# One decoder layer, prompt and decode together: meta tokens as keys and values only

## The chip, the cores and the metric

The kernel runs on one core of a Trainium2 chip, as one program that its author wrote out engine by engine, with semaphores by hand. The metric is the device time of one launch in microseconds. Engines are named as the profile names them: PE (TensorE, matmuls), PEld (its weight loads), ACT (ScalarE), DVE (VectorE), POOL (GpSimd, here mostly a DMA issuer), SP (SyncE, the other DMA issuer).

## The reference

One layer, D = 2048, 16 query heads and 4 key/value heads of 128, for two groups of tokens that share the weights: a prompt of 512 tokens with 16 learned meta tokens in front of it (528 positions), and 8 decode tokens with paged caches of 2048 positions each.

```
h = rmsnorm(x);  sq,sk,sv, fq,fk,fv, fl, g_sb,g_fx = split(h @ w_in)     # 12 parts of one projection
fq, fk = rmsnorm per head;  log_f = log_sigmoid(fl + b)
o_sb = stick_breaking(sq, sk, sv)      # strictly causal: exp(log_sigmoid(z) + suffix sum of -softplus(z))
o_fx = softmax(fq fk' * s + cum_q - cum_k) fv      # causal, bias from cumulative log forget
x += (sigmoid(g_sb) * o_sb + sigmoid(g_fx) * o_fx) @ w_out
x += relu(rmsnorm(x) @ w_up)^2 @ w_down            # D_FF = 8192
outputs: y for the 512 prompt tokens (y_prompt = x[:, 16:]) and the 8 decode tokens;
         sk, sv, fk, fv, log_f for all 528 prompt positions and the 8 decode tokens
```

The results that belong to a meta token alone (its queries, gates, attention output, residual, feed-forward) are not among the outputs. Its keys, values and forget logs are outputs, and all prompt queries attend to them.

## The kernel before, in words

All 536 tokens (16 meta, 512 prompt, 8 decode) lie along the free axis of every activation, features along partitions. A weight slab is 2048 x 128 (or, for the down projection, 1024 x 256), loaded in 1 MB by SP, split by ACT (`split_hi`) and DVE (`split_lo`) into a rounded high part and a rest, both float32r. A product is three matmuls into one PSUM bank (`split3`: high*high, low*high, high*low). `dense` runs a slab: 16 row blocks by two halves of HT = 268 columns, so 96 matmuls. The down projection's slab has the same count.

The stages, in PE's order:

- load and transpose x, first norm, four key/value groups of four slabs (`keys_values`), the forget slab, the first query slab;
- 16 stick-breaking heads (m = 0), then 16 forgetting heads (m = 1), function `head` on each engine. A head has one slab of the next head's queries (sq) and one of its own gates (sg), and between parts of these the attention: `scores` for five query tiles of 128 rows (aligned to position 0, so tile 0 has the meta tokens and the last tile 16 rows), each against `KW[i]` keys, with a floor of 256 columns; a bf16 mask matmul on the diagonal block; for m = 1 two more matmuls that add the forget bias. ACT and DVE turn scores into weights in `Z` (the stick-breaking chain in two parts, `Z_PARTS`: tiles 0 to 2 and tiles 3 and 4). `turn` transposes `Z` in six groups of blocks of at most 128 x 128; ACT and DVE split each group out of PSUM (`pa_hi`, `pa_lo`, `pb_hi`, `pb_lo`). `values` multiplies them with V: query tiles 0 and 1 as 256 columns over 2 key blocks, tiles 2 to 4 as 272 columns over 5;
- the decode tokens' attention over their caches (not touched);
- `wout`, the second norm, and eight chunks of the feed-forward (up slabs, down slabs), all through the same split products; at the end 20 transposes of four per 128 tokens and the stores.

`s_free`, `s_ok`, `pt_ps`, `pt_hi`, `pt_lo`, `o_ok` count how far PE, ACT and DVE are with a head; each engine takes its instructions strictly in written order, so an engine that waits holds all behind it.

Of the kernel before, what the change touches and what calls it, by code (L numbers as in the profile page):

```python
# [23 lines left out]
AX_X = mybir.AxisListType.X  # L24

# [11 lines left out]
HT = T // 2  # L37
KT = D // P
# [62 lines left out]
def build(nc, x_prompt, x_sample, cache_sb_k, cache_sb_v, cache_fox_k, cache_fox_v, cache_fox_logf,  # L101
# [3 lines left out]
    with ctx:  # L105
# [9 lines left out]
        xT_dram = nc.dram_tensor("xT_dram", [P, KT, T], F32).ap()  # L115
        kT_dram = nc.dram_tensor("kT_dram", [2 * NKV, P, TP], F32).ap()
        start_dram = nc.dram_tensor("start_dram", [1, 4], F32).ap()
        mg_dram = nc.dram_tensor("mg_dram", [2 * NH, P, TP], F32).ap()
# [44 lines left out]
        qraw = sb("qraw", [P, T], where=early)  # L163
        kraw = sb("kraw", [P, TP], where=early)
        vraw = sb("vraw", [P, TT, HD], where=early)
        q_hi = sb("q_hi", [P, TT * P], F32R, early)
        q_lo = sb("q_lo", [P, TT * P], F32R, early)
# [6 lines left out]
        pa_hi = sb("pa_hi", [P, 2, QA], F32R, early)  # L174
        pa_lo = sb("pa_lo", [P, 2, QA], F32R, early)
        pb_hi = sb("pb_hi", [P, TT, QB], F32R, early)
        pb_lo = sb("pb_lo", [P, TT, QB], F32R, early)
        gate = sb("gate", [P, T], where=early)
        mg = sb("mg", [P, TP], where=early)
        prev = sb("prev", [P, TP], where=early)  # L180
        mx = sb("mx", [P, TT], where=early)
        den = sb("den", [P, TT], where=early)
        rden = sb("rden", [P, TT], where=early)
# [34 lines left out]
        mraw = sb("mraw", [P, KT, T], where=a4)  # L218
        a4.close()
        a5 = ExitStack()  # L220
        n2_sq = [sb(f"n2_sq{k}", [P, T], where=a5) for k in range(2)]
        n2_t = [sb(f"n2_t{k}", [P, T], where=a5) for k in range(2)]
        n2_rs = sb("n2_rs", [P, T], where=a5)
        a5.close()
        u_hi = sb("u_hi", [P, FC // P, T], F32R, late)
        u_lo = sb("u_lo", [P, FC // P, T], F32R, late)
        r_sb = [sb(f"r_sb{k}", [P, T], where=late) for k in range(2)]
        m_hi = sb("m_hi", [P, KT, T], F32R, late)
        m_lo = sb("m_lo", [P, KT, T], F32R, late)
        x2T = sb("x2T", [P, KT, T], where=late)  # L230
# [80 lines left out]

        psf = ps[:, :, :].rearrange("p b n -> p (b n)")
# [7 lines left out]
        def z_tile(buf, i):  # L320
            return buf[:, ZO[i]:ZO[i] + KW[i]]

        def score_tile(i):
            b = (B_S + (i % 2 if i < 4 else 0)) * 512
            return psf[:, b:b + KW[i]]

        def pt_views(g):

            bank = B_PT + g % 2
            if g == 0:  # L330
                return [(ps[:, bank, 0:QA], pa_hi[:, 0, :], pa_lo[:, 0, :]),
                        (ps[:, bank, QA:QA + P], pa_hi[:, 1, P:QA], pa_lo[:, 1, P:QA])]
            j = g - 1
            c = (max(2, j) - 2) * P
            kw = P if j < 4 else LAST_P
            return [(ps[0:kw, bank, c:QB], pb_hi[0:kw, j, c:QB], pb_lo[0:kw, j, c:QB])]
# [18 lines left out]
        def _(sp):  # L355
# [86 lines left out]
            for t in range(TT):  # L442
                k = t % 2
                sp.wait_ge(y_a, 2 * t + 2)
                sp.wait_ge(y_v, 2 * t + 2)
                a = META if t == 0 else 0
                b = P if t < TT - 1 else LAST_P
                sp.dma_start(y_prompt[0, t * P - META + a:t * P - META + b, :], yn[k][a:b, :]).then_inc(y_st[k], 16)
                if t == TT - 1:
                    sp.dma_start(y_sample.rearrange("b o d -> (b o) d"), yn[k][LAST_P:LAST_ALL, :]).then_inc(y_st[k], 16)  # L450
            sp.wait_ge(y_st[0], 16 * 4)
# [4 lines left out]
        def _(pool):  # L456
# [20 lines left out]
            pool.dma_start(xT_dram, xT[:, :, :]).then_inc(xt_st, 16)  # L477
# [3 lines left out]
            for z in (q_hi, q_lo):  # L481
                pool.memset(z[:, T:TT * P].bitcast(F32), 0.0).then_inc(masks, 1)
            for z in (v_hi, v_lo):
                pool.memset(z[:, TT - 1, :].bitcast(F32), 0.0).then_inc(masks, 1)
            for z in (pa_hi, pa_lo):
                pool.memset(z[:, 1, 0:P].bitcast(F32), 0.0).then_inc(masks, 1)
            for z in (pb_hi, pb_lo):
                pool.memset(z[:, 3, 0:P].bitcast(F32), 0.0).then_inc(masks, 1)
                pool.memset(z[:, 4, :].bitcast(F32), 0.0).then_inc(masks, 1)
# [26 lines left out]
            def load_kv(m, n):  # L516
                v = (o_sv, o_fv)[m]
                pool.dma_start(kraw[:, :], kT_dram[bass.ds(n + m * NKV, 1)].rearrange("o p t -> (o p) t")).then_inc(kv_ld, 16)
                pool.dma_start(vraw[:, 0:TT - 1, :], v[0, 0, 0:SEQ].rearrange("(t p) n d -> p t n d", p=P)[
                    :, :, bass.ds(n, 1), :].rearrange("p t n d -> p t (n d)")).then_inc(kv_ld, 16)  # L520
                pool.dma_start(vraw[0:LAST_P, TT - 1, :], v[0, 0, SEQ:TP, bass.ds(n, 1), :].rearrange(
# [61 lines left out]
            for k in range(4):  # L583
                pool.dma_start(mraw[:, 4 * k:4 * k + 4, 0:TP],
                               mg_dram[NH + 4 * k:NH + 4 * k + 4].rearrange("h p t -> p h t")).then_inc(m_ld[k], 16)
# [5 lines left out]
        def _(pe):  # L591
# [15 lines left out]
            def dense(s, half, hi, lo, evac, evac_n, part=(0, KT)):  # L607
# [31 lines left out]
            def norm_pe(j, sq):  # L639

                for k in range(KT):
                    pe.wait_ge(nrm[j]["sq"], k + 1)
                    for half in range(2):
                        mm = pe.matmul(ps[:, B_O + half, 0:HT], ones[:, :], sq[k % 2][:, half * HT:(half + 1) * HT],  # L644
                                       start=(k == 0), stop=(k == KT - 1))
                    mm.then_inc(nrm[j]["ss"], 1)

            norm_pe(0, n_sq)

            def head_norm_pe(src, N):  # L650

                pe.wait_ge(rk["sq"], N + 1)
                for half in range(2):
                    mm = pe.matmul(ps[:, B_O + half, 0:HT], ones[:, :], src[:, half * HT:(half + 1) * HT],  # L654
# [17 lines left out]
            def keys_values(n, units):  # L672
                for u in units:
                    s = Slab(u, n * 4, n * 2)
                    proj(s, 0)
                    if u == 1:
                        head_norm_pe(Z, n)
                    proj(s, 1)
# [4 lines left out]
            for k in range(0, KT, 2):  # L683
                pe.wait_ge(nrm[0]["lo"], k + 2)
                for half in range(2):
                    proj(Slab(0), half, (k, k + 2))
# [4 lines left out]
            for s in (Slab(S_FL), Slab(S_Q0)):  # L691
                proj(s, 0)
                proj(s, 1)
# [10 lines left out]
            def scores(m, i, H):  # L704

                w = max(KW[i], 256)
                pe.wait_ge(s_free, H * 5 + ((0, 0, 1, 2, 4)[i] + SFREE0))
                parts = [(B_S + (i % 2 if i < 4 else 0), 0, min(w, 512))] + ([(B_S + 1, 512, LAST_P)] if i == 4 else [])
                for bk, c0, wd in parts:
                    out = ps[:, bk, 0:wd]  # L710
                    diag = c0 == 512 or i < 4
# [7 lines left out]
                    if diag:  # L719
                        d0, dw = (i * P, P) if i < 4 else (0, LAST_P)  # L720
                        mm = pe.matmul(ps[:, bk, d0:d0 + dw], identb[:, :], (mask_sb, mask_fx)[m][:, 0:dw],
# [3 lines left out]
            def turn(g, H):  # L725

                pe.wait_ge(pt_lo, H * 6 + (g - 1 + FREE_PT))
# [1039 lines left out]
```

## Time and profile before

| what | value |
|---|---|
| median of 3 runs (lowest, highest) | 3726.23 us (3721.62, 3727.31) |
| profiled execution, first to last instruction (the page gives no other time of it) | 3723.1 us |
| PE busy | 3579.6 us, 96%, 26809 matmuls |
| PEld busy | 3414.6 us, 92% |
| DVE, ACT, POOL busy | 1644.7, 1359.4, 342.7 us |
| DMA | 430.75 MB, 116 GB/s |

PE's busy time is the union of its records, which overlap: a matmul of a stream is recorded with some 0.29 us but starts 0.12 us after the one before it. So the pace of a stream is read from the distance of starts, or from busy time divided by count in a stretch where PE never stops.

### The profile page before, as it was taken

Reading aid. Unit: us, or ns where it says so; the run is one execution under the profiler, and the core shown is the slowest. Engines: PE = TensorE matmul, PEld = TensorE weight load, DVE = VectorE, ACT = ScalarE, POOL = GpSimd, SP = SyncE. Lnnn points to the kernel's source line nnn. Section 1 sums busy time; section 2 is a strip of 40 time slices with the busy share of each in tenths; the row PEclk is TensorE's granted clock in tenths of the full one; section 3 lists DMA queues with packets and bytes.
Section 4 is the critical chain, followed back from the end, with each engine's and each line's share of the span. In section 5 each row is a group of like instructions: output and inputs, shape, how many; then the busy total and the mean of one; then the engine's idle time right before and its main releaser. Section 6 shows DMA issues by size and latency. Waiting matters only on the chain.

```text
span 3723.1 us, 71770 instructions
## 1 busy us (share of the span) xinstructions
PE 3579.6 (96%) x26809; PEld 3414.6 (92%) x26809; DVE 1644.7 (44%) x2307; ACT 1359.4 (37%) x1917; POOL 342.7 (9%) x625
## 2 busy tenths in 40 slices
PE   6999999999999998998989989999999999999999
PEld 5999999999999987877779979999999999999998
DVE  3225666664444446666772243333333333333333
ACT  3224555554444444556651132222222221212121
POOL 0111111111111112222320000000000000000000
PEclk8999999999999999999999999999999999999999
DMA  4433333333332327667993222322232223223322
GB/s 151 115 108 96 84 95 94 89 81 91 88 98 83 96 58 236 219 212 250 319 329 101 79 57 91 89 90 81 90 89 88 82 90 88 89 82 90 89 87 84
DMA packets 480624, 430.75 MB, mean 116 GB/s; under 512 B 22145, under 2 KB 420354, under 8 KB 479250
## 3 DMA queue, kind: packets, MB, share of 16 engines
q1 hardware_dynamic: 441426, 311.74, 28.8%
q0 software_dynamic: 39136, 118.17, 9.6%
q8 instruction: 41, 0.67, 0.1%
q14 instruction: 21, 0.17, 0.0%
HBM read 405.95 MB, written 23.89 MB: 115 GB/s over the span
## 4 chain that ended last, share of the span: by engine, by line
PE 86%; DVE 6%; issue 4%; ACT 3%; DMA 1%; SPq 0%; ACTq 0%; DVEq 0%; POOL 0%; POOLq 0%
PE ps L603 27%; PE ps L604 26%; PE ps L605 26%; PE ps L813 3%; PE ps L738 1%; DVE E L1459 1%; DVE E L1453 1%; PE ps L644 1%; DVE n_t L1357 1%; DVE Z L1462 1%; PE ps L654 0%; PE ps L718 0%; PE ps L717 0%; ACT E L1129 0%; ACT E L1127 0%
## 5 line engine op out<-in xcount | busy, mean ns | idle before, releaser
L603 PE MATMUL ps<-h_hi,w_hi 128*128 128x268 f32 x2592 | 764.2, 295 | 13.2 <-DVE h_lo L1330 10.3
L603 PE MATMUL ps<-m_hi,w_hi 128*128 128x268 f32 x2560 | 735.8, 287 | 28.5 <-DVE m_lo L1330 11.0
L605 PE MATMUL ps<-h_lo,w_hi 128*128 128x268 f32 x2592 | 744.9, 287 | 0.0
L604 PE MATMUL ps<-h_hi,w_lo 128*128 128x268 f32 x2592 | 743.9, 287 | 0.0
L605 PE MATMUL ps<-m_lo,w_hi 128*128 128x268 f32 x2560 | 735.0, 287 | 0.0
L604 PE MATMUL ps<-m_hi,w_lo 128*128 128x268 f32 x2560 | 733.3, 286 | 0.0
L1005 ACT ACTIVATE w_hi<-w_raw 128x2048 fp32r<-128x2048 f32 x225 | 429.7, 1910 | 772.9 <-PE ps L605 762.0
L1330 DVE TENSOR_TENSOR w_lo<-w_raw,w_hi 128x2048 fp32r<-128x2048 f32 x225 | 515.4, 2291 | 356.7 <-ACT w_hi L1005 353.7
L603 PE MATMUL ps<-u_hi,w_hi 128*128 128x268 f32 x2048 | 584.3, 285 | 5.7 <-ACT r_sb L1287 5.7
L604 PE MATMUL ps<-u_hi,w_lo 128*128 128x268 f32 x2048 | 587.0, 287 | 0.0
L605 PE MATMUL ps<-u_lo,w_hi 128*128 128x268 f32 x2048 | 586.8, 287 | 0.0
L603 PEld LDWEIGHTS ps<-m_hi,w_hi 128*128 128x128 f32 x2560 | 485.0, 189 | 32.2 <-issue 15.8
L603 PEld LDWEIGHTS ps<-h_hi,w_hi 128*128 128x128 f32 x2592 | 491.9, 190 | 18.1 <-DVE h_lo L1330 12.0
L604 PEld LDWEIGHTS ps<-h_hi,w_lo 128*128 128x128 f32 x2592 | 491.4, 190 | 0.7
L605 PEld LDWEIGHTS ps<-h_lo,w_hi 128*128 128x128 f32 x2592 | 489.6, 189 | 0.0
L604 PEld LDWEIGHTS ps<-m_hi,w_lo 128*128 128x128 f32 x2560 | 484.7, 189 | 0.0
L605 PEld LDWEIGHTS ps<-m_lo,w_hi 128*128 128x128 f32 x2560 | 482.7, 189 | 0.0
L603 PEld LDWEIGHTS ps<-u_hi,w_hi 128*128 128x128 f32 x2048 | 385.9, 188 | 7.4 <-issue 6.7
L604 PEld LDWEIGHTS ps<-u_hi,w_lo 128*128 128x128 f32 x2048 | 385.4, 188 | 0.0
L605 PEld LDWEIGHTS ps<-u_lo,w_hi 128*128 128x128 f32 x2048 | 384.3, 188 | 0.0
L1684 DVE TENSOR_TENSOR x2T<-x2T,ps 128x268 f32 (+1 forms) x288 | 124.3, 432 | 527.6 <-PE ps L605 527.6
L1330 DVE TENSOR_TENSOR pg_lo<-ps,pg_hi 128x512 fp32r<-128x512 f32 x256 | 173.2, 689 | 105.8 <-ACT pg_hi L1190 105.6
(255 smaller groups left out, 4501.0 us busy)
## 6 DMA issues: line engine op xcount, KB each, us to landing
w_raw<-in_w_in_dram SPq DMA_DIRECT2D x81, 1024.0 KB, 5.9
w_raw<-in_w_up_dram SPq DMA_DIRECT2D x64, 1024.0 KB, 6.3
w_raw<-in_w_down_dram SPq DMA_DIRECT2D x64, 1024.0 KB, 5.4
w_raw<-in_w_out_dram SPq DMA_DIRECT2D x16, 1024.0 KB, 5.8
kraw<-kT_dram POOLq DMA_DIRECT2D x32, 264.0 KB, 3.1
mg_dram<-mg POOLq DMA_DIRECT2D x32, 264.0 KB, 2.3
vraw<-out_dram POOLq DMA_DIRECT2D x32, 256.0 KB, 3.3
pg<-in_cache_sb_k_dram SPq DMA_DIRECT2D x32, 256.0 KB, 3.0
```

What stands on the lines that cost most here:

```text
L603: pe.matmul(out, whi, xhi, start=first, stop=False)
L604: pe.matmul(out, wlo, xhi, start=False, stop=False)
L605: return pe.matmul(out, whi, xlo, start=False, stop=last)
L644: mm = pe.matmul(ps[:, B_O + half, 0:HT], ones[:, :], sq[k % 2][:, half * HT:(half + 1) * HT], start=(k == 0), stop=(k == KT - 1))
L738: mm = pe.transpose(ps[0:kw, bank, c:c + r], Z[0:r, ZO[i] + j * P:ZO[i] + j * P + kw], ident[0:r, 0:r])
L813: mm = pe.transpose(ps[:, 2 + n, r * P:(r + 1) * P], pg[b % 4][:, r, n * P:(n + 1) * P], ident[:, :])
L1005: act.activation(w_hi[nxt.slot][:, :, :], w_raw[nxt.slot][:, :, :], ACT.Copy).then_inc(w_hi_ok, 1)
L1330: return dve.tensor_tensor(out, a, hi.bitcast(F32), ALU.subtract)
L1357: dve.scalar_tensor_tensor(out=tmp[k % 2][:, :], in0=src[:, k, :], scalar=gain[:, k:k + 1], in1=rs[:, :], op0=ALU.mult, op1=ALU.mult).then ...
L1453: dve.scalar_tensor_tensor(out=E[:, a:b], in0=Z[:, a:b], scalar=0.0, in1=E[:, a:b], op0=ALU.max, op1=ALU.add).then_inc(z_sp, 1)
L1459: dve.tensor_tensor_scan(E[:, rev], ones[:, 0:1].to_broadcast([P, KW[i]]), E[:, rev], 0.0, ALU.mult, ALU.add).then_inc(z_scan, 1)
L1684: dve.tensor_tensor(v, v, ps[:, B_DENSE + half, 0:HT], ALU.add).then_inc(evac_v, 1)
```

## The change

Every matmul that doesn't produce keys, values or forget logs leaves the meta tokens out: TQ = 520 columns in two halves of HQ = 260, starting at column 16 of the first norm's output and at column 0 of everything after attention. The query tiles are aligned to the prompt: four of 128 rows, with 144, 272, 400 and 528 keys; the last one's scores take two banks of 264. The floor of 256 columns is gone. `Z` has 1344 columns instead of 1808. The weights are transposed in four groups (14 blocks), three for prompt keys, the last for the 16 meta keys of all four tiles; V is loaded with the prompt rows in blocks 0 to 3 and the meta rows in block 4. `values` becomes one accumulation in one bank, over columns j*128 to 512 for prompt block j and over all 512 for the meta block, and starts after the last group has been split. The wait for the second part of the stick-breaking weights moves from before `turn(1)` to before `turn(2)`.

```diff
+TQ = SEQ + NB
+HQ = TQ // 2
+QT = SEQ // P
-KW = [128, 256, 384, 512, 528]
-ZO = [0, 128, 384, 768, 1280]
-ZW = 1808
+KW = [META + (i + 1) * P for i in range(QT)]
+ZO = [sum(KW[:i]) for i in range(QT)]
+ZW = sum(KW)
-QA, QB = 256, 272
+KH = KW[3] // 2
+NPT = 4
...
+        def pt_blocks(g):
+            if g == 0:
+                return [(i, META, P, i * P) for i in range(3)]
+            if g == 1:
+                return [(1, META + P, P, 0), (2, META + P, P, P), (2, META + 2 * P, P, 2 * P)]
+            if g == 2:
+                return [(3, META + j * P, P, j * P) for j in range(4)]
+            return [(i, 0, META, i * P) for i in range(4)]
...
-            def dense(s, half, hi, lo, evac, evac_n, part=(0, KT)):
+            def dense(s, half, hi, lo, evac, evac_n, part=(0, KT), first=0, n=HQ):
...
-                    mm = split3(ps[:, B_DENSE + half, 0:HT], w_hi[s.slot][:, k, :], w_lo[s.slot][:, k, :],
-                                hi[:, k, half * HT:(half + 1) * HT], lo[:, k, half * HT:(half + 1) * HT],
-                                k == 0, k == KT - 1)
+                    cols = slice(first + half * n, first + (half + 1) * n)
+                    mm = split3(ps[:, B_DENSE + half, 0:n], w_hi[s.slot][:, k, :], w_lo[s.slot][:, k, :],
+                                hi[:, k, cols], lo[:, k, cols], k == 0, k == KT - 1)
...
+            def proj_all(s, half, part=(0, KT)):
+                dense(s, half, h_hi, h_lo, evac_a, s.banks + (half - 1 + FREE_DENSE), part, 0, HT)
             def proj(s, half, part=(0, KT)):
-                dense(s, half, h_hi, h_lo, evac_a, s.banks + (half - 1 + FREE_DENSE), part)
+                dense(s, half, h_hi, h_lo, evac_a, s.banks + (half - 1 + FREE_DENSE), part, META, HQ)
...
             def scores(m, i, H):
-                w = max(KW[i], 256)
-                pe.wait_ge(s_free, H * 5 + ((0, 0, 1, 2, 4)[i] + SFREE0))
-                parts = [(B_S + (i % 2 if i < 4 else 0), 0, min(w, 512))] + ([(B_S + 1, 512, LAST_P)] if i == 4 else [])
+                pe.wait_ge(s_free, H * QT + ((0, 0, 1, 3)[i] + SFREE0))
+                parts = [(B_S + i % 2, 0, KW[i])] if i < 3 else [(B_S, 0, KH), (B_S + 1, KH, KH)]
...
             def values(H):
                 pe.wait_ge(mg_ok, H + MG0)
-                pe.wait_ge(pt_lo, H * 6 + (1 + FREE_PT))
+                pe.wait_ge(pt_lo, H * NPT + (NPT + FREE_PT))
                 pe.wait_ge(hv_lo, H + 1)
-                for j in range(2):
-                    mm = split3(ps[:, B_O, 0:QA], v_hi[:, j, :], v_lo[:, j, :], pa_hi[:, j, :], pa_lo[:, j, :],
-                                j == 0, j == 1)
-                mm.then_inc(o_ok, 1)
-                for j in range(TT):
-                    pe.wait_ge(pt_lo, H * 6 + (j + 2 + FREE_PT))
-                    mm = split3(ps[:, B_O + 1, 0:QB], v_hi[:, j, :], v_lo[:, j, :], pb_hi[:, j, :], pb_lo[:, j, :],
-                                j == 0, j == TT - 1)
+                for j in range(QT + 1):
+                    c = j * P if j < QT else 0
+                    mm = split3(ps[:, B_O, c:SEQ], v_hi[:, j, :], v_lo[:, j, :], pt_hi_sb[:, j, c:SEQ], pt_lo_sb[:, j, c:SEQ],
+                                j == 0, j == QT)
                 mm.then_inc(o_ok, 1)
...
                 scores(m, 1, H)
                 proj(d, 0, (0, k1))
                 scores(m, 2, H)
+                proj(d, 0, (k1, k2))
                 scores(m, 3, H)
-                proj(d, 0, (k1, k2))
-                scores(m, 4, H)
                 proj(d, 0, (k2, KT))
...
                 turn(0, H)
+                turn(1, H)
+                proj(sg, 1, (0, KT // 2))
                 if m == 0:
                     pe.wait_ge(p_sb, H * 2 + 2)
-                turn(1, H)
-                proj(sg, 1, (0, KT // 2))
                 turn(2, H)
                 turn(3, H)
                 proj(sg, 1, (KT // 2, KT))
-                turn(4, H)
-                turn(5, H)
...
```

`keys_values` and the forget slab now call `proj_all` (268 columns as before). All buffers, evacuations, norms and stores on ACT, DVE, POOL and SP follow the new shapes; the last stage has four full token tiles and one of the 8 decode tokens.

## Rows read from the trace of the kernel before

**Rows 1.** Windows: us; PE, PEld, DVE, ACT, POOL busy (count); clock; DMA share, GB/s.
```profile
303.00:832.00 529.00, 518.85 (x3980) 491.17 (x3978) 327.25 (x449) 303.01 (x481) 73.80 (x130) 0.99 0.33 90
832.00:1400.00 568.00, 561.41 (x4236) 531.34 (x4236) 266.61 (x579) 261.72 (x509) 84.08 (x144) 0.99 0.31 85
2200.00:3705.00 1505.00, 1491.77 (x12041) 1488.49 (x12039) 497.31 (x626) 335.81 (x371) 0.00 (x0) 1.00 0.29 86
```
**Rows 2.** Costliest groups of the page: the first of three matmuls of each product.
```profile
L603 PE MATMUL ps<-h_hi,w_hi 128*128 128x268 f32 x2592 | 764.2, 295 | 13.2 <-DVE h_lo L1330 10.3
L603 PE MATMUL ps<-m_hi,w_hi 128*128 128x268 f32 x2560 | 735.8, 287 | 28.5 <-DVE m_lo L1330 11.0
L603 PE MATMUL ps<-u_hi,w_hi 128*128 128x268 f32 x2048 | 584.3, 285 | 5.7 <-ACT r_sb L1287 5.7
```
**Rows 3.** Timeline of PE, one stick-breaking head's end and the next one's scores.
```profile
470.19 0.46 PE L738 MATMUL ps<-ident,Z 128*128 128x128 f32 x3
470.58 0.39 PE L603 MATMUL ps<-pa_hi,v_hi 128*128 128x256 f32 x1
...
471.40 0.29 PE L603 MATMUL ps<-pb_hi,v_hi 128*128 128x272 f32 x1
...
473.28 0.28 PE L603 MATMUL ps<-k_hi,q_hi 128*128 128x256 f32 x1
...
474.15 0.37 PE L603 MATMUL ps<-h_hi,w_hi 128*128 128x268 f32 x1
474.36 0.28 PE L604 MATMUL ps<-h_hi,w_lo 128*128 128x268 f32 x1
...
475.72 0.34 PE L603 MATMUL ps<-k_hi,q_hi 128*128 128x384 f32 x1
...
476.25 0.23 PE L721 MATMUL ps<-mask_sb,identb 128*128 128x128 bf16 x1
...
477.10 0.37 PE L603 MATMUL ps<-h_hi,w_hi 128*128 128x268 f32 x1
...
478.67 0.39 PE L603 MATMUL ps<-k_hi,q_hi 128*128 128x512 f32 x1
...
479.37 0.17 PE L603 MATMUL ps<-k_hi,q_hi 128*128 128x16 f32 x1
479.40 0.26 PE L604 MATMUL ps<-k_hi,q_lo 128*128 128x16 f32 x1
...
479.66 0.37 PE L603 MATMUL ps<-h_hi,w_hi 128*128 128x268 f32 x1
```
**Rows 4.** Timeline of PE, a norm's matmuls over full float32 (two instructions each).
```profile
858.36 1.07 PE L654 MATMUL ps<-kvT,ones 128*128 128x268 f32 x4
```
**Rows 5.** Timeline of PE, transposes of a stick-breaking head and what follows them.
```profile
494.58 0.87 PE L738 MATMUL ps<-ident,Z 128*128 128x128 f32 x6
495.38 0.39 PE L603 MATMUL ps<-h_hi,w_hi 128*128 128x268 f32 x1
...
498.90 1.13 PE L738 MATMUL ps<-ident,Z 128*128 128x128 f32 x6 [0.30 <-DVE pa_lo L1330]
499.96 0.39 PE L603 MATMUL ps<-h_hi,w_hi 128*128 128x268 f32 x1
```
**Rows 6.** Timeline of PE, transposes of the last stage.
```profile
3713.72 1.97 PE L985 MATMUL ps<-ident,x2T 128*128 128x128 f32 x16 [2.62 <-ACT yn L1313]
3716.16 1.92 PE L985 MATMUL ps<-ident,x2T 128*24 128x128 f32 x16 [0.48 <-ACT yn L1313]
```
**Rows 7.** Timeline of DVE, second part of the stick-breaking chain in that head.
```profile
487.83 2.37 DVE L1459 TENSOR_TENSOR_SCAN E<-ones,E 128x512 f32<-128x512 f32 x2
490.24 1.24 DVE L1462 TENSOR_TENSOR Z<-Z,E 128x1040 f32<-128x1040 f32 x1
```
**Rows 8.** Timeline of DVE and PE, a forgetting head before its third group of transposes.
```profile
1041.34 0.62 DVE L1330 TENSOR_TENSOR pa_lo<-ps,pa_hi 128x256 fp32r<-128x256 f32 x2 [0.52 <-ACT pa_hi L1154]
...
1042.32 1.08 PE L738 MATMUL ps<-ident,Z 128*128 128x128 f32 x6
```

More of the change, by code:

```diff
@@ L173, in build @@
         E = sb("E", [P, ZW], where=early)
[L174 to L183, printed above, removed]
+        pt_hi_sb = sb("pt_hi_sb", [P, QT + 1, SEQ], F32R, early)
+        pt_lo_sb = sb("pt_lo_sb", [P, QT + 1, SEQ], F32R, early)
+        gate = sb("gate", [P, TQ], where=early)
+        mg = sb("mg", [P, SEQ], where=early)
+        prev = sb("prev", [P, SEQ], where=early)
+        mx = sb("mx", [P, QT], where=early)
+        den = sb("den", [P, QT], where=early)
+        rden = sb("rden", [P, QT], where=early)
         early.close()
@@ L217, in build @@
         a4 = ExitStack()
-        mraw = sb("mraw", [P, KT, T], where=a4)
+        mraw = sb("mraw", [P, KT, TQ], where=a4)
         a4.close()
         a5 = ExitStack()
-        n2_sq = [sb(f"n2_sq{k}", [P, T], where=a5) for k in range(2)]
-        n2_t = [sb(f"n2_t{k}", [P, T], where=a5) for k in range(2)]
-        n2_rs = sb("n2_rs", [P, T], where=a5)
+        n2_sq = [sb(f"n2_sq{k}", [P, TQ], where=a5) for k in range(2)]
+        n2_t = [sb(f"n2_t{k}", [P, TQ], where=a5) for k in range(2)]
+        n2_rs = sb("n2_rs", [P, TQ], where=a5)
         a5.close()
[L225 to L230, printed above, removed]
+        u_hi = sb("u_hi", [P, FC // P, TQ], F32R, late)
+        u_lo = sb("u_lo", [P, FC // P, TQ], F32R, late)
+        r_sb = [sb(f"r_sb{k}", [P, TQ], where=late) for k in range(2)]
+        m_hi = sb("m_hi", [P, KT, TQ], F32R, late)
+        m_lo = sb("m_lo", [P, KT, TQ], F32R, late)
+        x2T = sb("x2T", [P, KT, TQ], where=late)
         late.close()
@@ L441, in _ @@
                              .rearrange("o p k n -> (o p) k n"))
-            for t in range(TT):
+            for t in range(QT + 1):
                 k = t % 2
@@ L685, in _ @@
                 for half in range(2):
-                    proj(Slab(0), half, (k, k + 2))
+                    proj_all(Slab(0), half, (k, k + 2))
             keys_values(0, range(1, 4))
@@ L689, in _ @@
                 keys_values(n, range(4))
-            for s in (Slab(S_FL), Slab(S_Q0)):
-                proj(s, 0)
-                proj(s, 1)
+            proj_all(Slab(S_FL), 0)
+            proj_all(Slab(S_FL), 1)
+            proj(Slab(S_Q0), 0)
+            proj(Slab(S_Q0), 1)
             pe.wait_ge(logf_ok, 1)
@@ L977, in _ @@
             pe.wait_ge(evac_v, 32 * NC + 32 + FREE_DENSE)
-            for t in range(TT):
-                r = rows(t)
+            for t in range(QT + 1):
+                r = yrows(t)
                 for q in range(4):
@@ L1088, in _ @@
             evac(s, 1, qraw, ACT.Copy, SCALE)
-            act.wait_ge(masks, 8 + 13)
+            act.wait_ge(masks, 8 + 7)
             act.wait_ge(kT_st[0], 16 * NKV)
@@ L1148, in head @@
                 evac(sg, 0, gate, ACT.Sigmoid)
[L1149 to L1150 removed]
+                for g in range(NPT):
+                    act.wait_ge(pt_ps, H * NPT + (g + 1))
                     views = pt_views(g)
@@ L1304, in _ @@
             ffn(NC - 1, True)
-            for g in range(0, 4 * TT, 2):
+            for g in range(0, 4 * (QT + 1), 2):
                 t, q = g // 4, g % 4
@@ L1367, in _, with head_normed @@
             dve.wait_ge(xt_st, 16)
-            def head_normed(buf, gain, rs, N):
+            def head_normed(buf, gain, rs, N, n):
                 dve.wait_ge(rk["rs"], N + 1)
-                dve.scalar_tensor_tensor(out=buf[:, :], in0=buf[:, :], scalar=gain, in1=rs[:, 0:T],
+                dve.scalar_tensor_tensor(out=buf[:, :], in0=buf[:, :], scalar=gain, in1=rs[:, 0:n],
                                          op0=ALU.mult, op1=ALU.mult).then_inc(rk["out"], 1)
@@ L1408, in _ @@
             dve.tensor_scalar(nck[:, :], nck[:, :], -1.0, None, ALU.mult).then_inc(cum_ok, 1)
-            dve.wait_ge(masks, 8 + 13)
+            dve.wait_ge(masks, 8 + 7)
             dve.wait_ge(cum_ok, 2)
@@ L1732, in _ @@
             ffn(NC - 1, True)
-            for g in range(1, 4 * TT, 2):
+            for g in range(1, 4 * (QT + 1), 2):
                 t, q = g // 4, g % 4
```

227 lines of the change are left out of this document (109 added, 118 removed).

## The prediction, made before the changed kernel was built or run

> **What bounds the kernel now.** I read the busy times by stage first, then the costliest groups, then PE's timeline through one head, then what DVE does ahead of PE's waits. In the feed-forward stage PE is busy 1491.77 of 1505 us, in the two kinds of heads 518.85 of 529 and 561.41 of 568, while DVE and ACT lie between a fifth and two thirds [rows 1]. The granted clock is 1.00 and 0.99 there, the upper level of 2.4 GHz, so there is next to nothing to win from the clock. PE's own instructions set the time, and the question is what each costs in a stream. 1491.77 us over 12041 matmuls is 0.1239 us for a product matmul of 268 columns. The recorded 0.285 to 0.295 us [rows 2] are lives that overlap; they don't add up to time.
>
> The timeline gives the pace at other widths, by distance of starts [rows 3]: 256 columns 0.120 (470.58 to 471.40 is six, of which the first starts the second 0.10 late, as any product behind a short bf16 or full-float32 matmul does: 474.15 to 474.36 is 0.21 where 0.12 is usual); 272 columns 0.1253 (471.40 to 473.28, 15 of them); 384 columns 0.177 (475.72 to 476.25, three); 512 columns 0.233 (478.67 to 479.37, three). At 16 columns it does not go on falling: 479.40 to 479.66 holds two such and a mask of about 0.04, so 0.11 each. Pace follows the columns above 256, and there is a floor of 0.11 below.
>
> **Dense products.** Of the 81 slabs of the first projection (2592 / 32 [rows 2]), 17 keep 268 columns; 64 x 96 = 6144 matmuls get 260. So do all 3 x 2560 on m and 3 x 2048 on u: 19,968 in all. Eight columns less are worth 2.7 ns by the step from 256 to 272 (0.33 ns a column), 3.3 ns at one column per cycle of 2.4 GHz, 3.6 ns by the step from 272 to 384 and to 512 (0.44 to 0.46). The ends are 54 and 72 us. I take 3.1 ns, near the neighbours in width: -62 us. All of it lies on the path, since PE doesn't stop there.
>
> The Trainium skill (TensorE: Matmul & The Clock Gate, Back-to-back issue gap) gives N/2.4 + 2.5 ns for a warm matmul: 114 for 268 columns, where the rows show 124, and 3.33 ns less for 260; by that rule this term would be -67. The level differs from the trace, the step doesn't decide much.
>
> **Scores.** Before, a stick-breaking head spends 0.87 + 1.38 + 0.99 us (473.28 to 474.15, 475.72 to 477.10, 478.67 to 479.66 [rows 3]) plus three late starts of 0.09: 3.51. After: 3 x 0.11 for 144 columns, 3 x 0.125 for 272, 3 x 0.184 for 400 (0.177 and 16 more columns at 0.44 ns), 6 x 0.123 for the two of 264, and four masks with their late starts at 0.13: 2.51. That is 1.00 less. A forgetting head adds two matmuls to each piece: before 2 x (0.12 + 0.12 + 0.177 + 0.233 + 0.233 + 0.11) = 1.99, after 2 x (0.11 + 0.125 + 0.184 + 0.123 + 0.123) = 1.33, so 1.66 less. 16 x (1.00 + 1.66) = -43 us.
>
> The trace has no rounded matmul between 16 and 256 columns. From below the 144-column piece costs the floor, from above what full float32 costs: 1.07 us for four instructions of 268 columns, less the last one's 0.39, is 0.227 each and 0.85 ns a column [rows 4], and a matmul of that kind is two instructions. So 144 columns cost 0.11 or 0.24, 128 columns 0.11 or 0.215. The 16-column row is recorded once per matmul and stands at the floor, and the 256-column one is at 0.120; I take the floor and keep the other end as a rival.
>
> **Transposes.** Before, per head: 0.80 (494.58 to 495.38) for five wide blocks and one of the 16-row tile, 1.06 (498.90 to 499.96) for four and two, 0.39 (470.19 to 470.58) for one and two, and three late starts of 0.10: 2.55 [rows 3, 5]. The step from the first to the second says that a 16-row block costs 0.26 more than a wide one. After: 14 blocks of 128 rows. A wide one costs (1.97 - 0.27) / 15 = 0.113, and with only 24 columns to load (1.92 - 0.27) / 15 = 0.110 [rows 6], so the four meta blocks with 16 are no dearer. 14 x 0.113 = 1.58, with two late starts 1.78 if these stay. -0.77 to -0.97 a head; I take -0.9: -29 us. The bounds are -25 and -31.
>
> **Values.** Before 2.70 (470.58 to 473.28 [rows 3]). After, three each of 512, 384, 256, 128 and 512 columns: 3 x (0.233 + 0.177 + 0.12 + 0.11 + 0.233) = 2.62 and one late start of 0.10: 2.72. Nothing, or +10 us over 96 of the 128-column ones at the price of full float32.
>
> **Waits.** In the stick-breaking heads PE stands 0.30 us before the third group of transposes, until DVE has split the first [rows 5]. Ahead of that lies ACT's and DVE's chain through the head. Its second part loses 512 of 1040 columns: the two scans of 2.37 and the subtraction of 1.24 [rows 7] become about 1.2 and 0.65, and the last scores end 1 us earlier. So the chain ends some 3.5 us or more earlier, PE comes 2.5 to 3, and the 0.30 should go: -4.5 us over 15 heads. The moved wait gives that chain half a gate slab more. In the forgetting heads DVE is done at 1041.96 and PE comes at 1042.32, 0.36 later [rows 8]. Between the norm's matmuls and this point PE loses 48 x 3 ns and a narrow block, some 0.3 us, the other engines only a few per cent of their widths. A stall of 0 to 0.4 is likely there: +3 us. The new wait of `values` for all four groups has 24 dense matmuls ahead of it, 2.9 us. Behind it on PE stand the next head's scores, and for those ACT and DVE wait. The two groups that PE turns before these 24 take ACT and DVE about 2.3 us (two copies, two subtractions of 512 columns, at DVE's 0.62 for 384 [rows 8] some 0.8 each at most, one engine behind the other). It should be hidden; if not, it is a rival below. Net of all waits: -1.5 us.
>
> Narrower work on ACT, DVE and POOL lies beside PE and is set at nothing: if it were the bound, the dense gain would show only in part. The serial stretch of the second norm and the last stores are not in the sum.
>
> **Sum.** -62 - 43 - 29 + 0 - 1.5 = -135.5, so the profiled span of 3723.1 becomes 3587.6. It lies 3.1 below the median of the runs; I keep that difference: 3590.7, say **3591 us**, 3.6% less.
>
> **Rivals.**
>
> Narrow pieces at the pace of full float32. The code kept every rounded matmul of the heads at 256 columns or more except those of 16, which the floor covers, so the trace cannot exclude it. Price: 128 x 0.13 us for the 144-column pieces (three in 16 heads, five in 16) and 96 x 0.105: 16 + 10 = +26, 3617 us. Chance 14%.
>
> Weight loads set the dense pace. PEld is busy 1488.49 us of the same 1505, as full as PE [rows 1]. Then eight columns fewer are worth nothing: 3653. Against it: the same 128 x 128 load goes with 0.11, 0.120, 0.125, 0.177 and 0.233 us, by columns [rows 3]. Chance 4%. The Trainium skill (Trainium Kernel Development and Optimization, Performance Expectations) holds that the weight loads' busy share, not the matmuls', tells how close a kernel is to its limit; read so, this change would gain nothing in the feed-forward. The trace speaks against it as a reading of pace.
>
> The chain of ACT and DVE sets the stick-breaking heads, and doesn't shorten as I think. The stall of 0.30 says that the two are level now. If the chain keeps its length, PE waits for what it gained there, 16 x (1.0 + 0.9 + 0.6 + 0.3) = 45: 3636. Against it rows 7, whose columns are halved. Chance 6%.
>
> Slower than before: the new wait of `values`. If ACT reaches the last two groups only after other work (its gate evacuation and table load stand near them in its order), PE stands in every head before `values`, and all engines' next head with it. It has to be 135 / 32 = 4.2 us a head beyond the cover of 2.9 to undo the gain. At 5 us the time is 3591 + 160 = 3751. Nothing in the rows shows ACT or DVE that late at this place. Chance 2%.
>
> **How the numbers follow.** Likeliest case 72%, with the ends of its terms: dense -72 to -54, transposes -31 to -25, waits 3 us either way: 3576 to 3606. The rest, 2%, is a gain beyond that. To leave out less than 2 in 10 I add the float32 rival and a few us for what isn't priced below: **3570 to 3622**. Some 0.2% (7 us) is what a measurement of this kernel can tell from no change. Faster by more than that holds in all cases but the last: 0.97; within 0.01; slower 0.02.
>
> **What would show it.** The product groups with 260 columns should start 0.1205 to 0.121 apart; the feed-forward from the first up slab to the last down slab should be some 38 us shorter (12,288 x 3.1 ns). Heads should take about 3 us less each. The 144- and 128-column matmuls should start 0.11 to 0.12 apart; 0.2 or more is the first rival. PE should show no wait for the last split group before `values`, and none at the third group of the stick-breaking heads. A dense pace that stays at 0.124 breaks the forecast.

## The result, and the profile of the changed kernel

The changed kernel takes 3562.81 us (median of 4 runs, 3560.43 to 3565.82) against 3723.93 for the kernel before in the same call: ratio 0.9563, 95% interval 0.9549 to 0.9576. It is 161 us faster. I had forecast 3591, 133 us below this median, with 3570 as the low end: right in sign and in where the time comes from, too small in size. The profiled span went from 3723.1 to 3564.3, 158.8 less, where the sum had 135.5. The profiled execution was the slowest of the four, so the medians moved a little more than the spans.

The first view is the windows of three stages (us; busy time and instruction count of PE, PEld, DVE, ACT, POOL; clock; DMA share, GB/s). It answers to [rows 1].

```profile
303.00:783.00 480.00, 475.92 (x3830) 465.47 (x3829) 290.74 (x389) 277.08 (x436) 73.49 (x130) 0.99 0.36 99
783.00:1290.00 507.00, 503.42 (x3982) 488.81 (x3980) 242.77 (x477) 251.01 (x442) 78.92 (x141) 1.00 0.34 94
2044.00:3544.00 1500.00, 1478.85 (x12283) 1474.31 (x12282) 521.58 (x665) 351.60 (x396) 0.00 (x0) 1.00 0.30 88
```

PE is still the engine that never rests, and the clock is the same upper level. In the feed-forward 1478.85 us now hold 12283 matmuls, 0.1204 us each; before it was 0.1239. The groups of the page say the same less clearly, because a recorded life overlaps its neighbours: against [rows 2] their means fell from 295, 287 and 285 ns to these.

```profile
L618 PE MATMUL ps<-h_hi,w_hi 128*128 128x260 f32 (+1 forms) x2592 | 758.1, 292 | 13.3 <-DVE h_lo L1333 10.4
L618 PE MATMUL ps<-m_hi,w_hi 128*128 128x260 f32 x2560 | 728.3, 284 | 27.2 <-DVE m_lo L1333 10.1
L618 PE MATMUL ps<-u_hi,w_hi 128*128 128x260 f32 x2048 | 578.2, 282 | 5.7 <-ACT r_sb L1290 5.7
```

The pace itself is read from a window that holds nothing but products on one operand. Here is such a window of the kernel before, on u, and then two of the changed kernel, on m and on u.

```profile
2265.37:2359.14 93.77, 93.77 (x760) 93.77 (x759) 31.48 (x40) 15.58 (x9) 0.00 (x0) 1.00 0.31 90
```

```profile
2244.79:2335.54 90.75, 90.75 (x760) 90.75 (x759) 31.23 (x38) 25.26 (x38) 0.00 (x0) 1.00 0.32 93
2337.78:2428.19 90.41, 90.41 (x760) 90.41 (x759) 31.23 (x40) 15.35 (x8) 0.00 (x0) 1.00 0.31 93
```

Each counts 760 matmuls; two of these began before the window opened, so the length is divided by 758, here and in the windows of the experiments: 123.7 ns before, 119.7 and 119.3 now. The forecast was 120.5 to 121.

Next PE's timeline at the end of a stick-breaking head and through the next one's scores, which answers to [rows 3, 5].

```profile
476.65 0.82 PE L749 MATMUL ps<-ident,Z 128*128 128x128 f32 x6
477.22 0.36 PE L618 MATMUL ps<-h_hi,w_hi 128*128 128x260 f32 x1
...
480.21 1.04 PE L749 MATMUL ps<-ident,Z 128*128 128x128 f32 x8
481.00 0.37 PE L618 MATMUL ps<-h_hi,w_hi 128*128 128x260 f32 x1
...
483.97 0.40 PE L618 MATMUL ps<-pt_hi_sb,v_hi 128*128 128x512 f32 x1
...
485.84 0.45 PE L618 MATMUL ps<-pt_hi_sb,v_hi 128*128 128x512 f32 x1
486.12 0.39 PE L619 MATMUL ps<-pt_hi_sb,v_lo 128*128 128x512 f32 x1
486.35 0.40 PE L620 MATMUL ps<-pt_lo_sb,v_hi 128*128 128x512 f32 x1
486.58 0.23 PE L618 MATMUL ps<-k_hi,q_hi 128*128 128x144 f32 x1
486.65 0.28 PE L619 MATMUL ps<-k_hi,q_lo 128*128 128x144 f32 x1
486.76 0.28 PE L620 MATMUL ps<-k_lo,q_hi 128*128 128x144 f32 x1
486.88 0.23 PE L739 MATMUL ps<-mask_sb,identb 128*128 128x128 bf16 x1
```

No row carries a bracket, so PE waits for nothing here: the 0.30 ahead of the third group is gone, and `values` starts at 483.97 without a wait. The 144-column matmuls start 0.11 apart (the second only 0.07 behind the first), the floor and not full float32's pace. Fourteen transposes take 0.57 and 0.79 instead of the 2.25 of before's fifteen, and 483.97 to 486.58 is 2.61 for the values.

What the old stall ahead of the third group had cost is read from starts, because the bracket counts only from the recorded end of the product before it. In the kernel before, the third group starts at 498.90 [rows 5], and the product ahead of it at:

```profile
498.33 0.28 PE L605 MATMUL ps<-h_lo,w_hi 128*128 128x268 f32 x1
```

That is 0.58 where 0.12 to 0.13 is usual, so 0.45 and not 0.30, in each of 15 heads.

A new stall is in the forgetting heads; the view gives it no bracket. There the first narrow transpose starts 0.21 to 0.24 behind the last wide one, instead of 0.11. It waits until DVE has split the second group. In the head whose first narrow transpose starts at 939.56, this ends at 938.33 + 1.08 = 939.41:

```profile
938.33 1.08 DVE L1333 TENSOR_TENSOR pt_lo_sb<-ps,pt_hi_sb 128x384 fp32r<-128x384 f32 x3 [0.46 <-ACT pt_hi_sb L1157]
```

That is 0.10 a head.

Averaged over 12 heads of each kind, from the starts in the trace (us of PE for one head; "dense" includes a stall that follows a product):

| | scores | transposes | values | norm | dense | head |
|---|---|---|---|---|---|---|
| stick-breaking, before | 3.25 | 2.25 | 2.70 | | 24.64 | 32.83 |
| stick-breaking, after | 2.19 | 1.37 | 2.61 | | 23.49 | 29.67 |
| forgetting, before | 5.23 | 2.20 | 2.71 | 0.71 | 24.39 | 35.24 |
| forgetting, after | 3.52 | 1.47 | 2.61 | 0.69 | 23.67 | 31.96 |

A head is 3.17 and 3.28 us shorter. The dense column also holds the late start of each product behind a short matmul; the one at the start of the old `values` is in the column of the values. By stages, from first to last product start, the heads save 51.7 and 52.7, the output projection 5.4 and the feed-forward 48.8; the rest is within 1.6 us of before.

### The profile page after: what moved, and what is told of

Its sections match the earlier page's. It is cut to its first block, busy times and chain, and to the rows that moved or that the text cites. A ratio compares the mean times of both kernels' runs of the same rounds, so it can differ in the third digit from the quotient of the medians.

```text
span 3564.3 us, 70213 instructions
## 1 busy us (share of the span) xinstructions
PE 3428.4 (96%) x26425; PEld 3296.4 (92%) x26425; DVE 1582.9 (44%) x2147; ACT 1321.0 (37%) x1805; POOL 342.1 (10%) x619
## 4 chain that ended last, share of the span: by engine, by line
PE 92%; DVE 3%; ACT 1%; issue 1%; DMA 1%; SPq 1%; POOLq 0%; POOL 0%; ACTq 0%; DVEq 0%
PE ps L618 29%; PE ps L620 28%; PE ps L619 28%; PE ps L816 3%; PE ps L749 1%; PE ps L662 1%; DVE n_t L1360 1%; DVE pg_lo L1333 1%; DMA pg<-in_cache_sb_v_dram 1%; PE ps L672 0%; PE ps L735 0%; PE ps L736 0%; DMA xn<-in_x_prompt_dram 0%; DVE h_lo L1333 0%; ACT pg_hi L1241 0%
## 5 line engine op out<-in xcount | busy, mean ns | idle before, releaser
L618 PE MATMUL ps<-h_hi,w_hi 128*128 128x260 f32 (+1 forms) x2592 | 758.1, 292 | 13.3 <-DVE h_lo L1333 10.4
L618 PE MATMUL ps<-m_hi,w_hi 128*128 128x260 f32 x2560 | 728.3, 284 | 27.2 <-DVE m_lo L1333 10.1
L620 PE MATMUL ps<-h_lo,w_hi 128*128 128x260 f32 (+1 forms) x2592 | 737.5, 285 | 0.0
L619 PE MATMUL ps<-h_hi,w_lo 128*128 128x260 f32 (+1 forms) x2592 | 737.2, 284 | 0.0
L620 PE MATMUL ps<-m_lo,w_hi 128*128 128x260 f32 x2560 | 726.5, 284 | 0.0
L619 PE MATMUL ps<-m_hi,w_lo 128*128 128x260 f32 x2560 | 725.1, 283 | 0.0
L618 PE MATMUL ps<-u_hi,w_hi 128*128 128x260 f32 x2048 | 578.2, 282 | 5.7 <-ACT r_sb L1290 5.7
L619 PE MATMUL ps<-u_hi,w_lo 128*128 128x260 f32 x2048 | 577.7, 282 | 0.0
L620 PE MATMUL ps<-u_lo,w_hi 128*128 128x260 f32 x2048 | 577.3, 282 | 0.0
L1686 DVE TENSOR_TENSOR x2T<-x2T,ps 128x260 f32 (+1 forms) x288 | 122.0, 424 | 495.9 <-PE ps L620 495.9
```

Of the source, the lines that this page charges most:

```text
L618: pe.matmul(out, whi, xhi, start=first, stop=False)
L619: pe.matmul(out, wlo, xhi, start=False, stop=False)
L620: return pe.matmul(out, whi, xlo, start=False, stop=last)
L1686: dve.tensor_tensor(v, v, ps[:, B_DENSE + half, 0:HQ], ALU.add).then_inc(evac_v, 1)
```

## The experiments

In all of them "pace" is the mean distance of starts of two consecutive products of one shape, over all distances below 160 ns, and "feed-forward" the time from the first up product's start to the last down product's.

**The rows of m and u 536 columns apart again** (the change had also put them 520 apart, since they hold 520 tokens now):

```
-        u_hi = sb("u_hi", [P, FC // P, TQ], F32R, late)
+        u_hi = sb("u_hi", [P, FC // P, T], F32R, late)[:, :, 0:TQ]
...
-        m_hi = sb("m_hi", [P, KT, TQ], F32R, late)
+        m_hi = sb("m_hi", [P, KT, T], F32R, late)[:, :, 0:TQ]
...
```

> The changed kernel with the rows of m and u in SBUF 536 long as before, of which the 260-column halves of the first 520 are used: only the pitch of the moving operand's rows is put back, in 13,824 products. Theory A, width alone: no change, 3563 us within 3, pace 0.1195. Theory B, the pitch brings 0.7 ns a product: +10 us, 3573 us, and the pace of m and u goes to 0.1203, that of the queries' and gates' products, whose rows are still 536 long (0.1201).

Measured 3571.76 us (3569.86 to 3575.09), ratio 0.9586 [0.9569, 0.9604]. Windows of products alone, on m and on u:

```profile
2240.92:2331.94 91.02, 91.02 (x760) 91.02 (x759) 31.23 (x38) 25.24 (x38) 0.00 (x0) 1.00 0.32 93
2147.04:2238.30 91.26, 91.26 (x760) 91.26 (x759) 31.23 (x40) 15.57 (x9) 0.00 (x0) 1.00 0.31 92
```

120.1 and 120.4 ns instead of 119.7 and 119.3, and a feed-forward of 1509.1 instead of 1501.1; the five profiled runs with the new rows and the same feed-forward lie between 1499.2 and 1503.0. So some 8 us of the gain (6 to 10) hang on the rows' place, which the prediction had not considered. The ratio's interval overlaps that of the changed kernel; it is the windows and the stage that carry this reading. The wider rows also move the buffers behind them, so this run doesn't separate distance from place. With the old rows eight columns are worth 3.3 ns in the feed-forward.

**Other widths.** The two halves get any width. Where it is over 260 they overlap and the surplus is not read; at 256 and 252 the down projection leaves out the last 4 and 8 columns of each half, so these two kernels don't compute the whole layer and serve for the pace alone.

```
+W_H, W_M, W_U = 260, 264, 256
+def span(half, w):
+    a = 0 if half == 0 else (TQ - w if w > HQ else HQ)
+    return a, a + w
...
-                    cols = slice(first + half * n, first + (half + 1) * n)
+                    cols = slice(first + c0, first + c1)
...
-                            a, b = half * HQ, (half + 1) * HQ
+                            a, b = span(half, HQ if half == 0 and t == 0 and u == 0 and isinstance(j, int) else W_U)
...
```

> The changed kernel with 264 columns in the output and up projections (halves overlapping by 8 columns) and 256 in the down projection (the last 4 columns of each half are left out of the products). It maps pace against width. Theory A, a straight step of about 0.5 ns a column between 256 and 272: 0.1216 at 264, 0.1176 at 256. Theory B, one column per cycle from 260 on: 0.1213 and 0.1179. Theory C, a jump between 264 and 268 (late starts that come only above some width): 0.1205 at 264. Time about 3563 + 7680 x 2 ns - 6144 x 2 ns = 3566 us.

> As the one before, with 272 columns in the output and up projections (overlapping by 24) and 252 in the down projection (8 columns of each half left out). Theory A, straight step of 0.5 ns: 0.1256 at 272, 0.1156 at 252. Theory B, one column per cycle: 0.1246 and 0.1163. Theory C, the jump lies between 264 and 268 and the step is flat elsewhere: 0.1246 to 0.1256 at 272; if the floor of the weight loads at 0.112 is felt early, 0.1175 at 252. Time about 3563 + 7680 x 6 ns - 6144 x 3.5 ns = 3588 us.

One time each, 3561.63 and 3584.41 us. Windows on m and on u, first with 264 and 256 columns, then with 272 and 252:

```profile
2242.45:2334.01 91.56, 91.56 (x760) 91.56 (x759) 31.24 (x38) 25.26 (x38) 0.00 (x0) 1.00 0.32 92
2336.25:2425.74 89.49, 89.49 (x760) 89.49 (x759) 31.23 (x40) 15.34 (x8) 0.00 (x0) 1.00 0.31 94
```

```profile
2251.55:2346.40 94.85, 94.85 (x760) 94.85 (x759) 31.24 (x38) 25.27 (x38) 0.00 (x0) 1.00 0.31 89
2348.65:2436.79 88.14, 88.14 (x760) 88.14 (x759) 31.24 (x40) 15.34 (x8) 0.00 (x0) 1.00 0.32 96
```

Over all their products the paces are 116.3 ns at 252 columns and 118.1 at 256 (on u), 120.85 at 264 and 125.15 at 272 (on m). From 256 to 272 that is 0.44 ns a column, not the 0.33 of the prediction: its 0.120 for 256 columns lies 2 ns above this stream.

**268 columns everywhere, on the new rows.** The same edit with the width 268 for h, m and u.

> The changed kernel, but every product on h, m and u gets 268 columns again (rows stay 520 long in m and u, 536 in h; the two halves then overlap by 16 columns and the surplus results are not read). Everything else stays as changed: 19,968 matmuls go back to the old width. Theory A (the whole extra gain of the products comes from the eight columns): pace 123.5 ns on h, m and u as before, +80 us, about 3642 us. Theory B (the eight columns give one column per cycle of 2.4 GHz, 3.33 ns, and the shorter rows of m and u give the rest): +66 us, about 3629 us, with paces of about 123.2 on m and 122.7 on u. Theory C (the eight columns give what I forecast, 3.1 ns): +62 us, 3625 us.

3636.93 us (3634.37 to 3643.5), ratio 0.9758 [0.9742, 0.9774]: 74 us more than the changed kernel, between two of the expected values and matching none. Some 4 us of it lie in the decode stage (from the last head's values to the first output product: 551.5 us against 547.2), which the edit doesn't touch. On m and on u:

```profile
2274.01:2367.81 93.80, 93.80 (x760) 93.80 (x759) 31.23 (x38) 25.27 (x38) 0.00 (x0) 1.00 0.31 90
2177.61:2271.42 93.81, 93.81 (x760) 93.81 (x759) 31.24 (x40) 15.57 (x9) 0.00 (x0) 1.00 0.30 90
```

That is 123.8, the pace of before, and the feed-forward takes 1549.9, before 1549.8. So at 268 columns the new rows are worth nothing; at 260 they are worth some 8 us. The two don't add: the second theory's idea that the shorter rows give a fixed 0.4 and 1.1 ns falls. What stands is that undoing the width takes back all of the feed-forward's gain.

**Rows at other distances, and the same rows elsewhere.**

```
-        u_hi = sb("u_hi", [P, FC // P, TQ], F32R, late)
+        u_hi = sb("u_hi", [P, FC // P, 544], F32R, late)[:, :, 0:TQ]
...
-        m_hi = sb("m_hi", [P, KT, TQ], F32R, late)
+        m_hi = sb("m_hi", [P, KT, 528], F32R, late)[:, :, 0:TQ]
...
```

> The changed kernel with the rows of m put 528 columns apart and those of u 544 apart instead of 520; widths, counts and order stay. Theory A (what counts is whether rows are a multiple of 64 bytes: 528 and 544 are, 520 and 536 are not): both m and u come out faster than 119.8 and 119.3 ns, or both slower than 120.1 and 120.4. Theory B (what counts is that a row is short): m about 120.0, u about 120.8, some +9 us, 3572 us. Theory C (the row pitch does nothing, and the 8 us with 536 had another cause): 3563 us.

3562.84 us (3562.29 to 3565.54). On m and on u:

```profile
2242.36:2332.82 90.46, 90.46 (x760) 90.46 (x759) 31.22 (x38) 25.26 (x38) 0.00 (x0) 1.00 0.32 93
2335.06:2425.77 90.71, 90.71 (x760) 90.71 (x759) 31.24 (x40) 15.34 (x8) 0.00 (x0) 1.00 0.32 93
```

Over all products m came out faster (119.4), u at 119.7, within the 119.3 to 119.8 that u shows from run to run where it is as changed. Neither "multiples of 64 bytes" nor "shorter is faster" is borne out; the time is that of the third theory, but m's pace did move.

```
+        pad = sb("pad", [P, 8], F32, late)
         u_hi = sb("u_hi", [P, FC // P, TQ], F32R, late)
```

> The changed kernel with 32 bytes left free ahead of all buffers of the feed-forward: rows of m and u stay 520 columns apart, but every one begins 32 bytes further on. Theory A (what differs between the row pitches is where in memory a row begins): the paces of m and u move by some tenths of a ns from 119.8 and 119.3, the time by up to 8 us either way, 3555 to 3571 us. Theory B (the pitch itself counts, not the place): paces within 0.05 ns of these, 3563 us.

3568.21 us (3567.0 to 3571.51), 4 to 5 more than the changed kernel in its two series. On m and on u:

```profile
2245.63:2336.50 90.87, 90.87 (x760) 90.87 (x759) 31.21 (x38) 25.25 (x38) 0.00 (x0) 1.00 0.32 93
2152.02:2243.05 91.03, 91.03 (x760) 91.03 (x759) 31.21 (x40) 15.56 (x9) 0.00 (x0) 1.00 0.31 93
```

119.9 and 120.1 ns. Five profiled runs of this study have the very same feed-forward (the changed kernel twice, and the three experiments below that change only the heads); in these m is at 119.78 or 119.79, u at 119.3 to 119.8, the stage at 1499.2 to 1503.0. Here it is 1504.0, just outside. So 32 bytes move the pace a little: the place of a row seems to count beside the distance, but the stage differs by less than a clear verdict needs.

**Rows of h 544 apart, of m 528** (`h_hi` and `h_lo` as [P, KT, 544], m as above, u as changed):

> The changed kernel with the rows of h 544 columns apart instead of 536, those of m 528 and those of u 520. If 536 is the one slow pitch of the four seen so far for 260 columns, h gains what u gained from 536 to 544 (0.7 ns) over 6,144 products, -4 us, and m the 0.4 ns seen at 528 over 7,680, -3 us: 3556 us. If only the place of the buffers counted in the earlier runs, h may go either way: 3556 to 3570 us.

3559.88 us (3558.69 to 3560.33), with h at 119.1 ns instead of 120.1, m at 119.4. It was repeated beside the changed kernel itself:

> The changed kernel as it is, beside the next run on the same chip: 3563 us, a ratio of 0.956 to 0.957 to the kernel before.

> The rows of h 544 columns apart and those of m 528, as tried once already. Theory A (the places of the rows are worth what the paces say, 1.0 ns over 6,144 products on h and 0.4 over 7,680 on m): 9 us below the changed kernel's median of this call, 3554 us. Theory B (the medians seen so far, 3559.9 against 3562.8, are the truth, and part of it comes back as waits in the heads): 3 us below. Rival (no difference): within 1 us.

The changed kernel took 3563.76 us (3560.74 to 3568.23), ratio 0.9565 [0.9552, 0.9578]; this one 3559.06 (3555.05 to 3560.28), 0.9549 [0.9536, 0.9562]. Two windows with products on h alone, first of the changed kernel, then of this one, each with 119 starts:

```profile
460.62:474.91 14.29, 14.29 (x121) 14.29 (x120) 9.88 (x12) 9.80 (x15) 3.98 (x7) 1.00 0.40 107
462.06:476.21 14.15, 14.15 (x120) 14.15 (x120) 9.74 (x12) 9.66 (x15) 3.98 (x7) 1.00 0.39 108
```

120.1 and 118.9 ns. All five of its runs lie below all five of the other, by 4.7 us at the median; the intervals overlap. It is the fastest version of the study. The paces would make it 9. The heads give 0.16 and 0.14 us each where 192 products by 1.0 ns are 0.19; in the forgetting heads part of it goes into the stall ahead of the narrow transposes, which grows to 0.12. And in both profiled runs with these rows the decode stage was some 5 us longer (551.7 and 551.2, against 546.0 to 547.6 in the ten other runs with 260 columns on h); why is open.

**No cover for the new wait.** The last two groups of transposes go directly ahead of `values`.

```
-                turn(2, H)
-                turn(3, H)
                 proj(sg, 1, (KT // 2, KT))
+                turn(2, H)
+                turn(3, H)
```

> The last two groups of transposes are moved behind the second half of the gate slab, so the 24 products that lay between them and the products with the values now lie ahead of them. Theory A (the new wait is real and hidden by these 24 products): in the changed kernel the last subtraction ends 1.75 us after the last transpose (481.00 to 482.75), so PE should stand some 1.75 us in each of the 32 heads, +56 us, about 3619 us. Rival (ACT or DVE reach these groups late for other work in their order, so that the wait is longer than that and the cover was nearly used up): 2.9 us or more a head, +93 us or more. Rival (the pieces overlap and no wait shows): 3563 us.

3620.82 us (3616.05 to 3623.1), +58. PE's timeline, then DVE's, and the line of PE's waits (total, times, longest):

```profile
492.29 1.03 PE L749 MATMUL ps<-ident,Z 128*128 128x128 f32 x8
494.88 0.50 PE L618 MATMUL ps<-pt_hi_sb,v_hi 128*128 128x512 f32 x1 [1.56 <-DVE pt_lo_sb L1333]
```

```profile
493.55 1.27 DVE L1333 TENSOR_TENSOR pt_lo_sb<-ps,pt_hi_sb 128x512 fp32r<-128x512 f32 x2 [4.86 <-ACT pt_hi_sb L1157]
```

```profile
PE ps L618 <- DVE pt_lo_sb L1333: 48.5, 31, 1.8
```

The bracket counts from the recorded end of the last transpose; by starts a head is 1.82 and 1.71 us longer. The first theory holds: the wait exists, is about 1.75 us, and the 24 products between 481.00 and 483.97, 2.97 us, hide it with 1.2 to spare.

**The moved wait put back.**

```
                 turn(0, H)
+                if m == 0:
+                    pe.wait_ge(p_sb, H * 2 + 2)
                 turn(1, H)
                 proj(sg, 1, (0, KT // 2))
-                if m == 0:
-                    pe.wait_ge(p_sb, H * 2 + 2)
                 turn(2, H)
```

> The wait for the second part of a stick-breaking head's probabilities goes back from ahead of the third group of transposes to ahead of the second, that is 24 products earlier; the rest stays as changed. Theory A (the chain of ScalarE and VectorE got so short that the moved wait is worth nothing): in the changed kernel that part is ready at 502.47 and TensorE comes to the transposes at about 506.3, 3.8 us later, so no change, 3563 us. Rival (the chain still sets the stick-breaking heads and the later wait is what took the old stall of 0.30 us away): 0.3 to 3 us a head, 3568 to 3611 us.

3564.69 us (3563.66 to 3566.55), stick-breaking heads 29.67 as before the edit: no change. The rows of the changed kernel behind it, ACT's last step of the chain and then PE's first two groups of transposes of that head:

```profile
501.83 0.64 ACT L1139 ACTIVATE Z<-Z 128x528 f32<-128x528 f32 x1 [1.77 <-DVE Z L1465]
```

```profile
506.32 0.82 PE L749 MATMUL ps<-ident,Z 128*128 128x128 f32 x6
```

The second part is ready at 502.47, 3.8 us before PE comes even to the first group, so neither place of the wait holds PE.

**The narrow transposes twice** (`pt_blocks(g) * 2` for the last group):

> The four transposes with 16 columns to load are issued twice in each head, 128 matmuls of 128 rows more in all; nothing else changes. Theory A (a narrow transpose costs the floor of 0.11 us like any other, as the forecast of the transposes holds): +14 us, about 3577 us. Rival (it costs what the trace shows between its starts, 0.088 us): +11 us, 3574 us. Rival (a 16-row block costs 0.26 us more than a wide one, as the step in the old heads seemed to say): +47 us, 3610 us.

3577.2 us (3573.78 to 3580.55), +14.4; the heads grow by 0.41 and 0.44, so 0.103 to 0.110 us for one. In the timeline the four wide and eight narrow ones take 1.23:

```profile
485.27 1.47 PE L749 MATMUL ps<-ident,Z 128*128 128x128 f32 x12
486.50 0.37 PE L618 MATMUL ps<-h_hi,w_hi 128*128 128x260 f32 x1
```

A transpose that loads 16 columns costs what a wide one does; in the stick-breaking heads of the changed kernel both kinds start 0.109 apart in the trace. The Trainium skill (TensorE: Matmul & The Clock Gate, LDWEIGHTS) says that a weight load takes its columns divided by 1.2 in ns; an estimate from that is 107 for 128 columns and 13 for 16. The 0.109 of wide transposes agrees with the first; the second doesn't show. What sets the floor of the narrow ones stays open.

## Why the prediction was right in kind and too small

**Dense products: the step that failed.** The prediction put 3.1 ns on each of 19,968 matmuls, -62 us with ends of 54 and 72. They gave about 75, 3 beyond the far end: 16 x (0.64 + 0.65) = 20.7 in the heads (192 products a head, from 268 columns on the new rows to 260), 5.4 in the output projection, 48.8 in the feed-forward where I had named 38. That is 3.75 ns each.

Two things were mis-sized. First the slope: "by the step from 256 to 272 (0.33 ns a column)" rested on 0.120 and 0.1253, read from six and fifteen starts in short pieces of one head [rows 3]. Averaged over all heads, and without the late first one, the same two kinds of matmul start 119.6 and 125.9 ns apart, 0.39 a column, and the streams on u and m give 118.1 and 125.15, 0.44. So the correction for the late first start was sound; the sample and the operand were not those of the stream. Nor is the slope even: 4 columns are worth 1.1 to 1.8 ns between 252 and 264, 2.9 from 264 to 268, 1.4 from there to 272 (252 and 256 measured on u, 264 and 272 on m). With old rows and new width this gives 3.3 to 3.4 ns on h, m and u, 67 us in all, inside the bounds.

Second the rows: the change also put the rows of m and u 520 apart, and at 260 columns that gave another 8 us; the run with the old distance, 3571.8, would have been inside the range, though by less than 2 us. I had looked at what each matmul computes and not at where its operand lies.

The Trainium skill (TensorE: Matmul & The Clock Gate, Back-to-back issue gap) gives N/2.4 + 2.5 ns for a warm matmul; an estimate from that is 3.33 ns for eight columns. With the rows 536 apart the runs agree (3.3 to 3.4); with the others they show 3.8 to 4.4. The same estimate puts 260 columns at 111 ns, which none of them reaches.

**Scores:** 16 x (1.05 + 1.70) = -44, forecast -43. **Transposes:** 0.89 and 0.73 a head by their own starts, -26. The forecast of -29 also counted one late start less. That one is real, but it shows in the values: before, `values` came right behind transposes and its second matmul started late, now it comes behind dense products. The doubled narrow ones confirm the price per block. The 0.26 that a 16-row block seemed to cost more in the old heads was not the load of few columns. **Values:** 0.08 and 0.10 a head, -3, is that late start. The matmuls themselves were forecast at 2.62 and take 2.61; the forecast had charged a late start of 0.10 to the new order, which has none.

**Waits:** as forecast, the stall at the third group went, and `values` waits for nothing. But by starts it was 0.45 and not 0.30, so -7 over 15 heads where the forecast had -4.5: the bracket is not the whole price of a wait, since a stream's starts lie 0.12 apart while its records run on for 0.28. The likely stall of 0 to 0.4 in the forgetting heads came, at 0.10 a head and ahead of the fourth group instead of the third, +1.6 instead of +3. It comes with PE being faster: with 268 columns the same transposes start 0.109 apart and there is no stall, with h at 119.1 ns it is 0.12.

Of the 23 us that the sum lacks, 13 are dense products, 4 the waits, and 1 each the scores and the transposes; the other 4 are remainders of single stages, under 2 us each. The remaining 5 of the 28 between 3591 and the measured median come from the step from span to median: the forecast added 3.1 us, and the profiled span of the changed kernel lies 1.5 above its median.

**The rivals.** Float32 pace for narrow pieces is excluded by the 0.11 between starts. That weight loads set the dense pace is excluded by six widths with the same load and six paces, while PEld stays as full as PE (1474.31 of 1500 us). The chain in the stick-breaking heads has 3.8 us of slack. The wait of `values` was priced and is covered; to undo the gain it would have to be more than four times as long.

**Left open:** why the place of the rows matters. Four distances and one shift gave 119.1 to 120.4 ns at 260 columns, in no order of length or alignment that I could find, and at 268 the distance did nothing. One thing is common to all: with the rows 536 apart h, m and u are all slowest (120.1, 120.1, 120.4), while 520, 528 and 544 gave 119.1 to 119.8. The shift by 32 bytes, with 520, gave 119.9 and 120.1, so distance alone doesn't settle it. Nor do I know why a third of the distances between starts are 125 ns or more at 268 columns and under 7% at 260.

## What to carry to other kernels

Where one engine streams without a pause, price a change of width from a clean run of that width in the same stream, not from a short piece on another operand: 2 ns in 120 put one end of the bound at 54 us, where the slope of the streams gives 70. A narrower buffer changes the operands' place as well as their number, and both ends of a bound should allow for it. A new wait is priced by the last producer's end against the work that lies in between, and that margin (here 1.2 us) can be tested by taking the cover away. A stall in a stream is priced by the distance of starts, not by the idle time that the profile shows: 0.45 against 0.30 here.

## What the runs showed that I had not expected

Row distances in the on-chip buffers move the pace of otherwise equal matmuls by up to 1 ns in 120: h goes from 120.1 to 119.1 with its rows 544 instead of 536 columns apart, u from 120.4 (536) to 119.3 to 119.8 (520), and this only at 260 columns. Between 264 and 268 columns there is a step of 3 ns. And u's pace differs by up to 0.5 ns between kernels whose feed-forward is the same, and between two executions of the changed kernel itself (119.3 and 119.7), while m's stays within 0.01, so single paces of u should not be read closer than that.
